# Norm offset added at the turned tiles, half of the opening splits made in the closing chunk, and a 288-column key product

## What is computed

```python
for l in range(DEPTH):                                   # 2 layers
    m = hybrid_mixer(x, w_in[l], w_out[l], ...)          # h = x @ w_in[l]; attention; mixed @ w_out[l]
    x = layer_norm(ALPHA * x + m, ln1_g[l], ln1_b[l])
    hdn = jnp.square(jax.nn.relu(x @ w_up[l]))
    x = layer_norm(ALPHA * x + hdn @ w_down[l], ln2_g[l], ln2_b[l])

def layer_norm(x, g, b):
    mu = jnp.mean(x, -1, keepdims=True)
    var = jnp.mean(jnp.square(x - mu), -1, keepdims=True)
    return (x - mu) * lax.rsqrt(var + LN_EPS) * g + b
```

## Time and profile before

| | us |
|---|---|
| median of three runs | 2459.38 (2459.02 to 2459.68) |
| the profiled execution | 2459.1 |
| its span in the trace | 2457.2 |
| TensorE busy | 2430.9 (99%) |
| VectorE busy | 1489.5 (61%) |
| ScalarE busy | 1110.9 (45%) |
| GpSimd busy | 65.4 (3%) |
| read from HBM | 452.33 MB, 186 GB/s over the span |

### The profile page before, as it was taken

One profiled execution on the slowest core, in us unless ns is written; L12 is line 12 of the kernel. 1 busy time (PEld: TensorE's weight loads), 2 busy tenths in 40 slices (PEclk: granted clock), 3 DMA queues, 4 the chain that ended last, 5 costly groups with the idle time before them and its releaser, 6 DMA issues.

```text
span 2457.2 us, 30005 instructions
## 1 busy us (share of the span) xinstructions
PE 2430.9 (99%) x12620; PEld 2067.2 (84%) x12620; DVE 1489.5 (61%) x1968; ACT 1110.9 (45%) x1485; POOL 65.4 (3%) x84
## 2 busy tenths in 40 slices
PE   9999999999999999999999999999999999999998
PEld 7888888878888888888878888888788888888886
DVE  5566666676556556466665766666765565555566
ACT  3444544444445344344444454543453443443443
POOL 2000000020000000000110000000200000000001
PEclk9999999999999999999999999999999999999999
DMA  8545555655665665555545555557555556555553
GB/s 295 173 162 174 170 171 165 239 179 189 202 198 189 195 193 188 190 188 189 188 157 172 174 169 172 166 163 248 176 189 190 188 190 197 190 191 193 189 190 119
DMA packets 229654, 457.94 MB, mean 186 GB/s; under 512 B 7408, under 2 KB 12272, under 8 KB 228368
## 3 DMA queue, kind: packets, MB, share of 16 engines
q1 hardware_dynamic: 227904, 444.89, 55.2%
q0 software_dynamic: 1616, 11.14, 1.2%
HBM read 452.33 MB, written 3.67 MB: 186 GB/s over the span
## 4 chain that ended last, share of the span: by engine, by line
PE 93%; DVE 4%; ACT 1%; DMA 1%; issue 0%; SPq 0%; DVEq 0%; ACTq 0%
PE pw L466 33%; PE pw L470 16%; PE pw L485 14%; PE pw L487 14%; PE pw L486 14%; DVE w_lo L990 1%; PE pa L542 1%; PE pa L618 1%; DVE y L1088 1%; PE pa L539 1%; ACT y L865 0%; DMA raw<-in_w_in_dram 0%; DVE act_a L1057 0%; DMA y<-in_x_dram 0%; ACT w_hi L757 0%
## 5 line engine op out<-in xcount | busy, mean ns | idle before, releaser
L990 DVE TENSOR_TENSOR w_lo<-raw,w_hi 128x1024 fp32r<-128x1024 f32 (+1 forms) x820 | 982.4, 1214 | 685.6 <-ACT w_hi L757 677.8
L757 ACT ACTIVATE w_hi<-raw 128x1024 fp32r<-128x1024 f32 (+1 forms) x820 | 847.6, 1046 | 999.2 <-PE pw L487 521.4
L466 PE MATMUL pw<-act_a,w_hi 128*128 128x512 f32 x3456 | 1090.5, 397 | 1.6 <-DVE w_lo L990 1.6
L470 PEld LDWEIGHTS pw<-act_a,w_lo 128*128 128x128 f32 x3456 | 650.0, 188 | 153.6
L470 PE MATMUL pw<-act_a,w_lo 128*128 128x256 f32 x3456 | 679.8, 278 | 0.0
L466 PEld LDWEIGHTS pw<-act_a,w_hi 128*128 128x128 f32 x3456 | 528.6, 189 | 3.4 <-DVE w_lo L990 1.8
L485 PE MATMUL pw<-w_hi,act_b 128*128 128x512 f32 x1216 | 474.3, 390 | 0.1
L487 PE MATMUL pw<-w_hi,act_b 128*128 128x512 f32 x1216 | 473.2, 389 | 0.0
L486 PE MATMUL pw<-w_lo,act_b 128*128 128x512 f32 x1216 | 473.1, 389 | 0.0
L487 PEld LDWEIGHTS pw<-w_hi,act_b 128*128 128x128 f32 x1216 | 228.2, 188 | 47.8
L486 PEld LDWEIGHTS pw<-w_lo,act_b 128*128 128x128 f32 x1216 | 228.3, 188 | 47.1
(11 more groups left out here) (152 smaller groups left out, 1101.3 us busy)
## 6 DMA issues: line engine op xcount, KB each, us to landing
raw<-in_w_up_dram SPq DMA_DIRECT2D x128, 1024.0 KB, 5.3
raw<-in_w_down_dram SPq DMA_DIRECT2D x128, 1024.0 KB, 5.1
raw<-in_w_in_dram SPq DMA_DIRECT2D x124, 1024.0 KB, 5.1
raw<-in_w_out_dram SPq DMA_DIRECT2D x32, 1024.0 KB, 5.2
raw<-in_w_in_dram SPq DMA_DIRECT2D x8, 512.0 KB, 10.7
work<-in_ln_g_dram POOLq DMA_DIRECT2D x4, 1024.0 KB, 4.8
work<-in_ln_b_dram POOLq DMA_DIRECT2D x4, 1024.0 KB, 7.1
raw<-in_w_in_dram SPq DMA_DIRECT2D x8, 288.0 KB, 3.6
```

Of the source, the lines that this page charges most:

```text
L466: nc.tensor.matmul(pw[:, b, :], hi[:, i, cols], act_a[:, k].rearrange("p a t -> p (a t)"), start=(k == 0), stop=False)
L470: last = nc.tensor.matmul(pw[:, b, SEQ:2 * SEQ], lo[:, i, cols], act_a[:, k, 0, :], start=False, stop=(k == KT - 1))
L757: nc.scalar.activation(unit_hi(c, u), raw[:, PAIR * u:PAIR * (u + 1), 0:WIDTH[c]], ACT.Copy) \
L990: V.tensor_tensor(unit_lo(c, u), raw[:, PAIR * u:PAIR * (u + 1), 0:WIDTH[c]], unit_hi(c, u).bitcast(F32), ALU.subtract).then_inc(lo_ready, 1)
```

## The change

It has three parts.

1. **Offset.** TensorE turns y as soon as the gain is in. The offset is added when the turned piece leaves PSUM: it is now a column of one number per partition (b_col), so take_x is four ScalarE instructions of 128 columns with a bias operand, and take_x_lo four on VectorE with a scalar operand. b_col is made once in layer 0: three small loads on SP's queue ahead of the IKW loads, one turn ahead of turn_k_idx, and one copy. The residual y gets its offset later, by VectorE (residual_offset, eight pieces of 512 columns): in the MLP beside the third chunk's splits, and in layer 1's mixer beside the last four splits of IKW and four of IDX0. GpSimd adds only the last norm's offset for tile 0. The six gain loads are issued after IDX0's loads instead of IKW's.
2. **Splits.** Units 0 to 3 of an opening chunk are split inside the closing chunk, between the steps of tile 0's norm. For that, homes change: unit 0 lies in a new buffer (park), units 1, 2 and 5 in act_b, units 3, 4, 6 and 7 in ring slots 0 to 3. Pieces 2 and 3 of tile 1 are taken inside open_block and no more beside the next chunk. Both turns of the hidden rows stand behind units 4 and 5 of the next chunk, and VectorE takes the first rows after unit 1 and the second after unit 3.
3. **Key product.** Both parts of an IKW unit lie side by side in w_hi (288 columns). TensorE makes one matmul of 288 columns with the high activations and one of 144 with the low ones, 64 in a chunk and token tile pair where there were 96; take_ikw copies one half and adds the other.

The core of the diff:

```diff
+        OPEN_HOME = [("park", 0, None), ("act_b", 0, 1), ("act_b", 1, 3), ("ring", 0, 4), ("ring", 1, 5), ("act_b", 2, 5),
+                     ("ring", 2, 6), ("ring", 3, 7)]
+        OPEN_IN_SLOT = [u for u, (where, _, _) in enumerate(OPEN_HOME) if where == "ring"]
...
+            slot = u % RING
+            if OPENING[c]:
+                where, slot, _ = OPEN_HOME[u]
+                if where == "park":
+                    return park[:, PAIR * lo:PAIR * (lo + 1)]
+                if where == "act_b":
+                    return act_b[:, LOAD * slot + PAIR * lo:LOAD * slot + PAIR * (lo + 1)].rearrange("p k a t -> p k (a t)")
+            if c % NC == IKW:
+                return w_hi[:, slot * PAIR:(slot + 1) * PAIR, lo * KW:(lo + 1) * KW]
+            return (w_lo if lo else w_hi)[:, slot * PAIR:(slot + 1) * PAIR, 0:WIDTH[c]]
         def unit_hi(c, u):
+            return unit_home(c, u, 0)
...
+                return c - N_OUT, UNITS - 1
             if CLOSING[c]:
-                if u < RING:
-                    return (c - N_OUT if c % NC == LAST_OUT else c - N_OUT, UNITS - 1)
                 return c - 1, u
-            if OPENING[c] and u >= RING:
-                return c - 1, UNITS - 1
+            if OPENING[c]:
+                v = OPEN_HOME[u][2]
+                return (c - 1, v) if v is not None else (-1, 0)
             if u >= RING:
                 return c, u - RING
-            return c - 1, u if c > 0 and OPENING[c - 1] else u + RING
+            return c - 1, OPEN_IN_SLOT[u] if c > 0 and OPENING[c - 1] else u + RING
...
+                        load_offsets()
                     for s in range(LOADS):
                         if layer == 0 and c == 0:
                             continue
                         load(layer * NC + c, s, in_v[layer, :, LOAD * s:LOAD * (s + 1), col:col + width])
-                    if layer == 0 and c == IKW:
+                    if layer == 0 and c == IDX0:
...
-                        if layer + 1 < DEPTH:
-                            add_offset(2 * layer + 1, t, j, x_ready)
-                        elif t == 0:
-                            add_offset(2 * layer + 1, t, j, out_ready[t][j])
+            n = 2 * DEPTH - 1
+            pool.wait_ge(ln_landed, 32 * (n + 1))
+            for j in range(LOADS):
+                pool.wait_ge(gained, norm_count(n, 0, j))
...
+            def ikw_unit(c, u):
+                pe.wait_ge(lo_ready, c * UNITS + u + 1)
+                for t in range(TT):
+                    b = BANKS[c][t]
+                    if u == 0:
+                        wait_bank(c, b)
+                    for i in range(PAIR):
+                        k = PAIR * u + i
+                        both = w_hi[:, u % RING * PAIR + i, 0:2 * KW]
+                        nc.tensor.matmul(pw[:, b, 0:2 * KW], act_a[:, k, 0, t * P:(t + 1) * P], both, start=(k == 0), stop=False)
+                        last = nc.tensor.matmul(pw[:, b, 0:KW], act_a[:, k, 1, t * P:(t + 1) * P], both[:, 0:KW],
+                                                start=False, stop=(k == KT - 1))
+                    if u == UNITS - 1:
+                        last.then_inc(bank_full[b], 1)
...
                         pe.wait_ge(a_ready, n - HC + 1)
                 else:
-                    pe.wait_ge(x_ready, norm_count(e - 1, t, j))
+                    pe.wait_ge(gained, norm_count(e - 1, t, j))
                     if t > 0:
...
-                                if (quarter, j, u) == (0, 1, 1):
-                                    turn_hidden(layer, 1)
+                                if (quarter, j) == (0, 1) and 4 <= u < 4 + TT:
+                                    turn_hidden(layer, u - 4)
                                 continue
                             if j == UPS:
...
+                    slot = (TT * j + t) % HC
+                    last = nc.scalar.activation(act_a[:, HC * j:HC * (j + 1), 0, t * P:(t + 1) * P],
+                                                pa[:, slot, :].rearrange("p (i t) -> p i t", i=HC), ACT.Copy)
+                else:
+                    for i in range(HC):
+                        k = HC * j + i
+                        last = nc.scalar.activation(act_a[:, k, 0, t * P:(t + 1) * P], pa[:, j, i * P:(i + 1) * P], ACT.Identity,
+                                                    bias=b_col[:, (e - 1) * KT + k:(e - 1) * KT + k + 1])
+                last.then_inc(a_hi, 1)
...
+                if not last:
+                    split_hi(c + 1, 0)
                 norm_seed(n, 0)
-                for j in range(LOADS):
-                    centre(n, 0, j)
+                if not last:
+                    split_hi(c + 1, 1)
+                centre(n, 0, 0)
+                centre(n, 0, 1)
+                if not last:
+                    split_hi(c + 1, 2)
+                centre(n, 0, 2)
+                centre(n, 0, 3)
+                if not last:
+                    split_hi(c + 1, 3)
             def open_block(c, n):
                 e = n + 1
-                split_hi(c, 0)
+                if n == 0:
+                    act.wait_ge(b_col_ready, 1)
                 take_x(e, 0, 0)
-                split_hi(c, 1)
-                split_hi(c, 2)
+                split_hi(c, 4)
                 take_x(e, 0, 1)
-                split_hi(c, 3)
-                take_x(e, 0, 2)
-                split_hi(c, 4)
-                take_x(e, 0, 3)
                 split_hi(c, 5)
                 norm_seed(n, 1)
+                take_x(e, 0, 2)
                 split_hi(c, 6)
-                centre(n, 1, 0)
+                take_x(e, 0, 3)
                 split_hi(c, 7)
-                for j in range(1, LOADS):
+                for j in range(LOADS):
                     centre(n, 1, j)
-                for j in range(2):
+                for j in range(LOADS):
                     take_x(e, 1, j)
...
+                            if layer == 0:
+                                act.wait_ge(b_turned, 1)
+                                nc.scalar.activation(b_col[:], pa[:, 3, SEQ:SEQ + (2 * DEPTH - 1) * KT], ACT.Copy) \
+                                    .then_inc(b_col_ready, 1)
                             nc.scalar.activation(k_idx_t[:], pa[:, 3, 0:SEQ], ACT.Copy).then_inc(kidx_sb, 1)
                         if (lc, u) == (IDX0 + 1, 1):
...
+                else:
+                    for i in range(HC):
+                        k = HC * j + i
+                        last = V.scalar_tensor_tensor(out=act_a[:, k, 1, t * P:(t + 1) * P], in0=pa[:, j, i * P:(i + 1) * P],
+                                                      scalar=b_col[:, (e - 1) * KT + k:(e - 1) * KT + k + 1],
+                                                      in1=act_a[:, k, 0, t * P:(t + 1) * P].bitcast(F32),
+                                                      op0=ALU.add, op1=ALU.subtract)
+                last.then_inc(a_ready, 1)
+            def residual_offset(n, i):
+                t, j = divmod(i, LOADS)
+                cols = slice(j * COLS, (j + 1) * COLS)
+                dve.wait_ge(gained, norm_count(n, t, j))
+                V.tensor_tensor(y[:, t, cols], y[:, t, cols], ln_b[:, cols], ALU.add).then_inc(offset_done, 1)
...
-                    V.tensor_copy(ikw[:, t, :], pw[:, b, 0:KW]).then_inc(bank_free[b], 1)
+                    did(V.tensor_copy(ikw[:, t, :], pw[:, b, KW:2 * KW]))
+                    steps.wait()
+                    V.tensor_tensor(ikw[:, t, :], ikw[:, t, :], pw[:, b, 0:KW], ALU.add).then_inc(bank_free[b], 1)
                     dve.wait_ge(bank_free[b], USES[c][b] + 1)
...
+                last = n == 2 * DEPTH - 1
+                if not last:
+                    split_lo(c + 1, 0)
                 add_to_y(c, N_OUT - 1, 0, True)
                 aggregate(0)
                 scales(n, 0)
-                for j in range(LOADS):
-                    gain(n, 0, j)
+                if not last:
+                    split_lo(c + 1, 1)
+                gain(n, 0, 0)
+                gain(n, 0, 1)
+                if not last:
+                    split_lo(c + 1, 2)
+                gain(n, 0, 2)
+                gain(n, 0, 3)
+                if not last:
+                    split_lo(c + 1, 3)
             def open_block(c, n):
                 e = n + 1
-                split_lo(c, 0)
+                if n == 0:
+                    dve.wait_ge(b_col_ready, 1)
                 take_x_lo(e, 0, 0)
-                split_lo(c, 1)
-                split_lo(c, 2)
-                take_x_lo(e, 0, 1)
+                split_lo(c, 4)
                 add_to_y(c - 1, N_OUT - 1, 1, True)
                 aggregate(1)
-                split_lo(c, 3)
+                take_x_lo(e, 0, 1)
+                split_lo(c, 5)
                 take_x_lo(e, 0, 2)
-                split_lo(c, 4)
-                take_x_lo(e, 0, 3)
-                split_lo(c, 5)
                 scales(n, 1)
                 split_lo(c, 6)
```

(36 more changed lines are left out.)

75 lines of the change are left out of this document (35 added, 40 removed).

## The result

The changed kernel takes 2441.35 us (median of four runs, 2441.05 to 2441.73), the kernel before in the same comparison 2459.47. The ratio is 0.9929, with a 95% interval of 0.9917 to 0.9941. So 18.1 us are gone between the medians (0.74%), where 14.2 were forecast. The time lies in the forecast range of 2440.5 to 2452.5, near its lower end. The profiled execution took 2441.05 us with a span of 2439.3, 17.9 less than the span before.

The account below looks back on a forecast made before the run. TensorE, busy 2430.9 of 2457.2 us, was taken as the bound. The terms 10.5 - 3.8 + 5.9 - 1.3 + 3.0 - 0.15 = 14.15 us gave 2459.4 - 14.2 = 2445.2 us, range 2440.5 to 2452.5.

Parts of the forecast that it names:

- The norms: At each of three norms, early splits and offset at the takes win 3.5 us, 10.5 in all; bounds 4.4 or 2.2 each.
- Rival 4: At the norms and the bank behind: cheap pieces (4.4 a norm) and a bank wait of 1 us, 2441; chance 0.06.
- Rival 1: At the norms: small pieces are dear (1.6 and 1.45 a take), norms give 2.2 each, 2449; chance 0.10.
- Rival 5: At the norms: everything hangs on VectorE; from 0.57 us a piece the gain is gone, at 0.65 2464; chance 0.03.
- nothing would be won at a norm: At the norms: the waits only move from GpSimd to VectorE, 2456; chance 0.03.
- The bank behind an MLP opening: In the chunk behind an MLP's opening, TensorE waits for its fourth bank: 1.8 + 0.1 lost at two norms, 3.8 us.
- rival 2: The clock falls in the new 1.8 us holes, and layer 0's low clock might stay: 2448 to 2450; chance 0.12.
- The residual adds: Eight adds of 0.68 each in the MLP's next chunk hide behind VectorE's slack; without that cover, 5.4 us a layer.
- The key product: 32 pairs of 288 and 144 columns take 7.75 us: 2.9 won per layer, 5.9 in both (bounds 4.3 and 7.2).
- The banks behind it in layer 1: Behind layer 1's key product, late take_ikw frees the third bank 0.9 us late, the fourth 0.1: -1.3 us.
- The start: In layer 0, moving gain loads lets the load behind the key product arrive in time, ending wait and low clock: 3.0 us.
- Rival 3: At the start the load still lands at 46.2; layer 0's 2.9 and 3.0 us go, clock suffers: 2452; chance 0.09.

Follow-up runs that it names:

- half pieces: The changed kernel with VectorE's takes in eight pieces of 64 columns instead of four of 128: 2447.69 us.
- the run with five orders: Changed kernel with residual adds later, tile 1's hidden rows ahead of split 2, its first piece turned a unit earlier and taken ahead of a gain: 2433.98 us.
- The run with later adds: The changed kernel with the first two residual adds of an MLP's third chunk moved to the fourth, the others shifted by two: 2440.34 us.
- the key product alone: The kernel before with the 288-column key product and two-step take_ikw, nothing else; gain loads stay where they were: 2457.17 us.
- Three changes of order: The changed kernel with hidden rows ahead of split 3, MLP residual adds later, and layer 1's adds behind the key product one unit later: 2437.01 us.

## Why the prediction was right, and where its size was off

**What bounds the kernel, what a norm costs.** Right. The losses sat where the idle table put them, and the experiments moved the time only there. That the loss at a norm is more than its idle column also holds: removing a wait of 0.56 gave 0.80.

**The norms: the mechanism right, the price of a take mis-sized.** Forecast 3.5 each, measured 4.9 to 5.0. VectorE is the full engine in tile 0 and five takes lie in its way, as the half pieces show. But I sized a take at 1.33 us, with bounds of 1.2 and 1.45, and it holds VectorE for 1.04 (0.26 a piece), outside the bounds. ScalarE's take I had at 1.25, and it is 1.0, within its bounds. Five takes by 0.29 are 1.45 us, about what a norm gave beyond the forecast. That the two agree so closely is in part luck, for the last of the five is no longer held up by VectorE's list: VectorE stood idle ahead of it.

```profile
519.70 1.13 DVE L1124 SCALAR_TENSOR_TENSOR act_a<-pa,b_col,act_a 128x128 fp32r<-128x128 f32 x4 [0.79 <-ACT act_a L832]
```

The wait that is left at tile 1's first unit is the length of the chain of turn, ScalarE and VectorE. That fits the run with five orders, where this piece is turned a unit earlier and taken ahead of a gain, and the wait is gone. The changed kernel's groups of pieces:

```profile
L832 ACT ACTIVATE act_a<-pa,b_col 128x128 fp32r<-128x128 f32 x96 | 27.3, 371 | 13.0 <-PE pa L550 13.0
...
L1124 DVE SCALAR_TENSOR_TENSOR act_a<-pa,b_col,act_a 128x128 fp32r<-128x128 f32 x96 | 26.8, 341 | 9.4 <-ACT act_a L832 9.1
```

The length was nearly right (0.341 for a row of 0.349). The mistake was to take length for pitch, the distance between two starts: neighbours overlap by 0.08 us on VectorE too, as I had allowed for ScalarE alone. A group of four is 0.28 x 4 long, and the next instruction starts 0.26 x 4 after it began. So of the three forecast waits (0.6, 0.5, 1.05) only the last is there, with 0.56. The Trainium skill, VectorE: DVE Perf Modes, The TRN2 errata, has this price in its table, in VectorE's row for a PSUM source: 120 cycles plus the columns, at 0.96 GHz. That is 0.258 for 128 columns, 0.192 for 64 and 0.658 for 512, estimates; measured pitches are 0.26, 0.19 (1.54 / 8) and 0.60 (512.90 to 513.50 in the kernel before). In the prediction I had cited another formula of that section, which the page gives for a tensor_tensor add and which makes 0.291, between the pitch and the length. The page's advice to tile from 512 elements up is true of the price, a take was 0.60 and is 1.04. Yet the advice would have been wrong here, for the small pieces took GpSimd's adds out of the way: with the old order of splits they still gained 1.7 us a norm.

**The rivals on the pieces.** Rival 4 (2441) came nearest to the time, by its cheap pieces alone: its short bank wait was not there. Rival 1 is refuted. Rival 5's slope is shown: at 0.19 x 8 a take, TensorE lost 2.2 us at each norm. Its threshold of 0.57 a piece was not tried. That nothing would be won at a norm (2456) falls with the 5 us that each norm gave.

**The bank behind an MLP opening.** Right to 0.1 us: 1.92 at each of the two, released by VectorE's hidden rows. The granted clock was 1.00 over both stretches with such a hole (501 to 545 and 1720 to 1764), so rival 2 falls.

**The residual adds.** Costed at nothing, wrong: 1.1 us, or 0.54 in each MLP. I argued with VectorE's mean slack in a unit, but the order at the chunk's boundary decides, where a bank waits. The run with later adds shows it.

**The key product.** Right: 0.242 us a pair, 7.74 us in both layers.

**The banks behind it in layer 1.** The add ahead of take_ikw was the main cause, as said; moving it gave 0.6 us. The loss was 0.85 instead of 1.3. VectorE's timeline there:

```profile
1253.61 0.69 DVE L1135 TENSOR_TENSOR y<-y,work 128x512 f32<-128x512 f32 x1
1254.21 0.30 DVE L1197 COPY ikw<-pw 128x144 f32<-128x144 f32 x1
1254.54 0.30 DVE L1199 TENSOR_TENSOR ikw<-ikw,pw 128x144 f32<-128x144 f32 x1
```

take_ikw starts 1.32 us after the product's end at 1252.89 (1245.15 + 7.74), where I had 1.65.

**The start.** Right: 3.0 us beside the key product's 2.9. ScalarE does still wait for later loads there (0.88 us at 44.00, 1.43 at 47.44), which I had named as a sign of being wrong, but TensorE does not wait for them. Rival 3 (the load stays late) falls. Its mechanism is real, though, as the key product alone shows: where the load is late, the 2.9 us don't count.

**The sum.** In the traces 17.9 us against 14.15: 4.4 more from the norms, 0.4 from the key's banks, -1.1 from the residual adds. That the total came within 4 us is in part luck, since the term put at nothing hid a quarter of what the norms gave beyond the forecast.

## What to carry to other kernels

Price short instructions by the distance between two starts in a chain, not by their length, and look at which operands lie in PSUM. A part that shortens work in front of a late transfer gives nothing until the transfer is moved; change both. When work is added to an engine with much mean slack, read the order at the place where a bank or a buffer is freed: at five places a split or an add that stood ahead of a releasing instruction (splits and a residual add in each MLP, one add behind the key product) cost this kernel most of 3.8 + 1.1 + 0.9 = 5.8 us of its gain. Three changes of order took 4.3 of them back.

## What was new about the hardware

- VectorE instructions that read one operand from PSUM follow each other every 0.19 us at 64 columns and 0.26 at 128 (scalar_tensor_tensor), and every 0.60 at 512 (tensor_tensor). ScalarE's pieces with a bias column follow every 0.25 at 128 columns (four from 510.24 to the next instruction at 511.23).
- VectorE's split (two operands in SBUF) goes from 1.22 to 2.31 us beside a GpSimd add. A take with one operand in PSUM keeps its 0.68.
- After a wait of 1.65 us with dense 512-column matmuls before it, the granted clock stayed at 1.00. After waits of 1.62 and 6.15 us that followed the key product it was 0.70 and 0.50 in the mean of 50 to 55 us. What makes the difference was not settled.
